# A two-layer decoder trunk on one core: HGRN operands formed two levels ahead, ScalarE reordered around the local softmax, the memory scaling moved to the local rope, the first two output tiles interleaved

## What is computed

```
hq,hf,hi,hg,rq,rk,rv,rg,sq,sk,sv,gates = split(rmsnorm(x) @ w_in)
A: HGRN2: f = lb+(1-lb)*sigmoid(hf); log_f = log(f); k = (1-lb)*sigmoid(-hf); q = silu(hq)
   o = gated linear recurrence (q, k, hi, cumulated log_f); rmsnorm(o) * silu(hg)
B: retention (q, k with rope, fixed decay); rmsnorm(o) * silu(rg)
C: sliding-window attention with rope, 128 wide, a sink per head
x += (g_a*A@w_a + g_b*B@w_b + g_c*C@w_c) @ w_out
x += cross_attention(rmsnorm(x), rmsnorm(mem))      # 256 memory tokens
x += peer_ffn(rmsnorm(x))                           # top-16 of product keys, 16384 experts
```

## Time and profile before

| | |
|---|---|
| runs, median (lowest to highest) | 2420.35 us (2418.95 to 2420.59) |
| the profiled execution's own time | 2419.26 us |
| its span, first to last instruction | 2417.5 us |
| TensorE busy | 2385.2 us, 99% |
| VectorE, ScalarE, GpSimd busy | 1646.6, 1318.2, 1097.3 us |
| chain that ended last | TensorE 89%, VectorE 8%, ScalarE 2% |

### The profile page before, as it was taken

How to read it: one execution, slowest core, us unless ns; L and a number is a source line. 1 busy time by engine, 2 the same in 40 slices (tenths; PEclk the granted TensorE clock), 3 DMA queues, 4 the chain that set the end, 5 groups by cost and what they waited for, 6 DMA issues and landing times.

```text
span 2417.5 us, 43862 instructions
## 1 busy us (share of the span) xinstructions
PE 2385.2 (99%) x15876; PEld 2168.0 (90%) x15876; DVE 1646.6 (68%) x3223; ACT 1318.2 (55%) x2048; POOL 1097.3 (45%) x452
## 2 busy tenths in 40 slices
PE   9999999999999999999999999999999999999999
PEld 8999888999999888888889898889999998888887
DVE  7467634879995556777664686258799946667776
ACT  5575555565555555554555655555555545555444
POOL 5776777787773000000067767767877730000000
PEclk9999999999999999999999999999999999999999
DMA  7544555456767667777654445544567776667775
GB/s 240 169 140 140 172 170 164 158 182 216 241 241 253 208 207 225 245 244 245 206 190 155 148 140 173 176 157 157 182 218 242 255 231 205 213 225 238 245 246 169
DMA packets 186554, 485.37 MB, mean 201 GB/s; under 512 B 14272, under 2 KB 81088, under 8 KB 181824
## 3 DMA queue, kind: packets, MB, share of 16 engines
q1 hardware_dynamic: 179808, 443.26, 55.4%
q10 hardware_dynamic: 6624, 40.44, 4.9%
HBM read 449.04 MB, written 34.60 MB: 200 GB/s over the span
## 4 chain that ended last, share of the span: by engine, by line
PE 89%; DVE 8%; ACT 2%; issue 1%; DMA 0%; SPq 0%; DVEq 0%
PE banks L894 29%; PE banks L493 13%; PE banks L495 13%; PE banks L494 13%; PE banks L836 5%; PE banks L522 5%; PE banks L865 3%; PE banks L837 3%; PE banks L523 2%; DVE arena L1692 1%; DVE arena L1738 1%; DVE arena L1690 1%; PE banks L797 1%; PE banks L781 1%; PE banks L762 1%
## 5 line engine op out<-in xcount | busy, mean ns | idle before, releaser
L423 POOL TENSOR_TENSOR w_lo<-ring,w_hi 128x1024 fp32r<-128x1024 f32 x448 | 1097.1, 2457 | 861.9 <-ACT w_hi L925 861.1
L925 ACT ACTIVATE w_hi<-ring 128x1024 fp32r<-128x1024 f32 x776 | 818.8, 1056 | 431.5 <-PE banks L894 338.6
L493 PE MATMUL banks<-h_r,w_hi 128*128 128x256 f32 x2464 | 702.5, 285 | 6.8 <-ACT arena L1000 5.6
L495 PE MATMUL banks<-h_r,w_lo 128*128 128x256 f32 x2464 | 697.0, 283 | 0.0
L494 PE MATMUL banks<-h_r,w_hi 128*128 128x256 f32 x2464 | 696.9, 283 | 0.0
L894 PE MATMUL banks<-w_hi,o_r 128*128 128x512 f32 x2048 | 559.8, 390 | 0.0
L493 PEld LDWEIGHTS banks<-h_r,w_hi 128*128 128x128 f32 x2464 | 472.0, 192 | 10.6 <-issue 8.8
L494 PEld LDWEIGHTS banks<-h_r,w_hi 128*128 128x128 f32 x2464 | 472.2, 192 | 0.6 <-issue 0.5
L495 PEld LDWEIGHTS banks<-h_r,w_lo 128*128 128x128 f32 x2464 | 472.1, 192 | 0.0
L894 PEld LDWEIGHTS banks<-w_hi,o_r 128*128 128x128 f32 x2048 | 380.0, 188 | 79.4
L1945 DVE TENSOR_TENSOR w_lo<-ring,w_hi 128x1024 fp32r<-128x1024 f32 x320 | 390.0, 1219 | 31.4 <-ACT w_hi L925 31.4
(11 more groups left out here) (303 smaller groups left out, 3219.6 us busy)
## 6 DMA issues: line engine op xcount, KB each, us to landing
ring<-in_stream SPq DMA_DIRECT2D x776, 512.0 KB, 3.3
gates_dram<-o_f ACTq DMA_DIRECT2D x32, 1024.0 KB, 5.5
o_f<-gates_dram SPq DMA_DIRECT2D x32, 1024.0 KB, 7.2
arena<-in_mem ACTq DMA_DIRECT2D x2, 1024.0 KB, 10.3
arena<-in_keys ACTq DMA_DIRECT2D x2, 1024.0 KB, 7.0
arena<-in_c_decay ACTq DMA_DIRECT2D x2, 768.0 KB, 5.0
x<-in_x SPq DMA_DIRECT2D x4, 256.0 KB, 5.8
out_dram<-arena SPq DMA_DIRECT2D x4, 256.0 KB, 2.1
```

The source lines that it names most:

```text
L423: pool.tensor_tensor(w_lo[:, s, :], ring[:, s, :], w_hi[:, s, :], ALU.subtract).then_inc(sem(f"low{s}"), 1)
L493: pe.matmul(out, lhs[0], rhs[0], start=first, stop=False)
L495: return pe.matmul(out, lhs[1], rhs[0], start=False, stop=last)
L925: act.activation(w_hi[:, s, :], ring[:, s, :], ACT.Copy).then_inc(sem(f"high{s}"), 1)
```

## The change

It has four parts. The core of the diff:

```diff
-        left = part(0, 4 * T)
-        right = part(1024, 4 * T)
-        operands = ((left, right), (part(7680, 4 * T), part(8704, 4 * T)))
+        operands = ((part(11776, 4 * T), part(6656, 4 * T)), (part(7680, 4 * T), part(8704, 4 * T)))
 # TensorE
+                def wide_two(g, n, src, pairs):
+                    for s, chunks in ((0, (0, 1, 2, 3, 4, 5)), (1, (0, 1, 2, 3)), (0, (6, 7)), (1, (4, 5, 6, 7))):
+                        if chunks[0] == 0:
+                            wait_tile(g, s)
+                            bank_free(n + s)
+                        for k in chunks:
+                            if k % 2 == 0:
+                                ev(pairs, k // 2 + 1, KC // 2)
...
                 group(G_RG, T_RG, feature_tile, hr)
+                if l == 0:
+                    pe.wait_ge(sem("angles"), 4)
+                    rms_sums(square, KC, sem("mem_squared"), 1, bank[:, 6, 0:T]).then_inc(sem("mem_summed"), 1)
...
                 token_group(G_HI, T_HI, hr)
                 ev("ret_out")
-                if l == 0:
-                    rms_sums(square, KC, sem("mem_squared"), 1, bank[:, 6, 0:T]).then_inc(sem("mem_summed"), 1)
...
-                with pe.Fori(0, 2) as i:
-                    for s in range(SLOTS):
-                        wide_tile(G_OUT + i, s, T_OUT + i * SLOTS + s, h_r, pairs=None if s else "mixed_low")
+                wide_two(G_OUT, T_OUT, h_r, "mixed_low")
+                for s in (2, 3):
+                    wide_tile(G_OUT, s, T_OUT + s, h_r)
+                group(G_OUT + 1, T_OUT + SLOTS, wide_tile, h_r)
 # ScalarE (the square and the root of the memory move to the retention gate, RG)
                 split_next(G_HI, 0)
                 window_exp(0)
-                split_next(G_HI, 1)
                 token_half(0, G_HI, P_HI, lambda t: hi[:, t, :])
-                split_next(G_HI, 2)
-                token_half(1, G_HI, P_HI, lambda t: hi[:, t, :])
+                token_half(1, G_HI, P_HI, lambda t: hi[:, t, :], split=False)
+                for s in range(1, SLOTS):
+                    split_next(G_HI, s)
                 copied(T_HI)
-                for n, (dst, src, scale) in enumerate(((cum, hf, 1.0), (kin, hf, -1.0), (qin, hq, 1.0))):
...
+                evac(G_HG, 0, hg[:, 0:1, :])
+                gate_sigmoid(cum, hf, 1.0)
+                gate_sigmoid(kin, hf, -1.0)
+                evac(G_HG, 1, hg[:, 1:2, :])
+                gate_sigmoid(qin, hq, 1.0)
                 window_turned(0)
-                evac_group(G_HG, by_feature(hg))
+                evac(G_HG, 2, hg[:, 2:3, :])
+                evac(G_HG, 3, hg[:, 3:4, :])
                 window_out(0)
...
+                gate_out(0)
+                ev("forget")
+                act.activation(cum, cum, ACT.Ln).then_inc(sem("log_forget"), 1)
+                gate_out(1)
+                window_exp(1, (0, 1))
+                gate_out(2)
+                window_exp(1, (2, 3))
+                gate_out(3)
+                level_exp(1)
+                gate_out(4)
+                gate_out(5)
+                window_turned(1)
+                gate_out(6)
+                level_exp(2)
+                gate_out(7)
+                window_out(1)
+                ahead_of = {0: 3, 3: 4, 5: 5, 7: 6, 9: 7, 10: 8}
                 for q in range(12):
-                    if q % 3 != 2:
-                        level_exp(q // 3 * 2 + 1 + q % 3)
+                    if q in ahead_of:
+                        level_exp(ahead_of[q])
                     gate_out(8 + q)
 # VectorE
                 dve.tensor_tensor(st, bank[:, 0:4, 0:3 * P], decay, ALU.mult).then_inc(sem("ret_decayed"), 1)
+                if l == 0:
+                    dve.wait_ge(sem("mem_rooted"), 1)
+                    link(dve.reciprocal(minv[:, :], minv[:, :]))
...
+                scaled_mem(range(KC // 2))
                 out_of_banks(T_HF)
...
                 rope(wqk, ...).then_inc(sem("win_roped"), 1)
+                scaled_mem(range(KC // 2, KC))
...
                 window_softmax(1, first_span)
+                level_operands(1)
+                level_operands(2)
                 window_low(1)
                 link(take_level(0))
+                for i in range(3, 9):
+                    link(take_level(i - 2))
+                    level_operands(i)
+                link(take_level(7))
```

More of the change, by code:

```diff
@@ L524, in wide_tile @@
                     m.then_inc(sem(f"slot{s}_used"), 1)
+                def wide_two(g, n, src, pairs):
[6 more added lines that the diff above has]
+                                ev(pairs, k // 2 + 1, KC // 2)
+                            hi, lo = weights(s, k)
+                            pe.matmul(wide_out(s), hi, src[:, :, k, :], start=(k == 0), stop=False)
+                            m = pe.matmul(tile_out(s), lo, src[:, 0, k, :], start=False, stop=(k == KC - 1))
+                        if chunks[-1] == KC - 1:
+                            m.then_inc(sem(f"slot{s}_used"), 1)
                 def token_group(g, n, src):
@@ L703, in level_across @@
                     ev("level_ready", 9, 9)
+                    lt, rt = operands[0]
                     for hd in range(HEADS):
-                        m = pe.matmul(bank[:, 2, hd * P:(hd + 1) * P], left[:, hd * T:hd * T + P],
-                                      right[:, hd * T + P:(hd + 1) * T], start=True, stop=True)
+                        m = pe.matmul(bank[:, 2, hd * P:(hd + 1) * P], lt[:, hd * T:hd * T + P],
+                                      rt[:, hd * T + P:(hd + 1) * T], start=True, stop=True)
                     m.then_inc(sem("level_scored"), 1)
@@ L1024, in by_feature, with token_half @@
                     return lambda n: dst[:, bass.ds(n, 1), :]
-                def token_half(t, g, n, dst):
+                def token_half(t, g, n, dst, split=True):
                     if t == 0:
@@ L1032, in token_half @@
                     act.activation(dst(t), bank[:, 4 + t, :], ACT.Copy).then_inc(sem("bank_free"), 1)
-                    if t:
+                    if t and split:
                         high_part(l * GROUPS + g + 1, SLOTS - 1)
@@ L1049, in _ @@
                 act.activation(cosb[:, 1, :], cosb[:, 1, :], ACT.Sin).then_inc(sem("trig"), 1)
+                if l == 0:
+                    act.wait_ge(sem("mem_summed"), 1)
+                    act.activation(minv[:, :], bank[:, 6, 0:T], ACT.Sqrt, bias=eps[:, :], scale=1.0 / D
+                                   ).then_inc(sem("mem_rooted"), 1)
                 copied(T_SQ)
@@ L1675, in first_span, with level_operands @@
                     span_of(1)
[L1677 to L1687 removed]
+                def level_operands(i):
+                    m = LEVELS[i]
                     ev("level_exp", 2 * i, 16)
@@ L1735, in _ @@
                 link(dve.tensor_tensor(summed, summed, hgs, ALU.mult))
-                ev("mem_loaded", 16, 16)
-                for k in range(KC):
-                    dve.scalar_tensor_tensor(mem[:, k, :], mem[:, k, :], gain["xkv"][:, k:k + 1], minv[:, :],
-                                             ALU.mult, ALU.mult).then_inc(sem("mn_made"), 1)
                 ev("hgrn_rooted")
```

47 lines of the change are left out of this document (14 added, 33 removed).

## The result

The changed kernel takes 2443.9 us (median, 2443.06 to 2445.03), the kernel before 2420.2 beside it: a ratio of 1.0099, 95% interval 1.0082 to 1.0117. It is slower by 23.7 us, where 9.7 were predicted, and lies above the predicted range. The profiled execution took 2445.03 us, its span is 2443.2.

The account below looks back on a forecast made before the run. TensorE, 99% busy, bounds the kernel, so only its waits move the time. +3.3 (moved matmuls) + 1.55 - 0.7 (HI to level 0) + 6.0 (loop) - 0.9 (BR1) = +9.25, plus 0.5 for clock: 2430 us, range 2408 to 2439.

Parts of the forecast that it names:

- two kinds: TensorE's waits: tiles waiting for ScalarE's copy out of a bank (5.6 us), levels waiting for VectorE's second operand (3.5 us).
- Part 1, the forget chain: Around the softmax: chain ends 37.5 us behind HI's start; HI to level 0 takes 59.6 us in each layer.
- The first wait: TensorE at gate tile 3 waits 3.1 us for its bank, freed behind the logarithm and `gate_out(1)`.
- the second: TensorE at gate tile 4 waits 3.15 us more, its bank freed behind half of the exponentials and `gate_out(2)`.
- Part 2, the memory: Moved sums of squares cost +3.3 us behind RG; BR1's third tile waits 0.45 us less, 0.9 in both layers.
- Part 3, the loop: Level loop with operands formed ahead: between -3.3 and +5.4 us, taken as +3.0 in each layer.
- ties: Level loop: +5.4 us if all go to GpSimd; half could go the other way, at 2.3 us each.
- The clock: TensorE's lower clock behind long waits: 0.5 us added in all.
- Part 4, the output tiles: Interleaved output tiles: the mixture's third low part is asked for at the same chunk, so 0 us, at most 0.1.
- My own rule from part 1: VectorE and GpSimd's port pair is locked for a whole instruction; a VectorE instruction with two SBUF inputs waits.
- (c): Rival: full collisions and the lower clock, both waits in one layer behind each other: +16.9 us, 2437; chance 0.13.
- (a): Rival: VectorE gets between GpSimd's instructions, neither gate tile waits, HI to level 0 takes 53.2 us, 2405; chance 0.2.

Follow-up runs that it names:

- g: Changed kernel with both interleaved output tiles' sums taken before VectorE's low parts of memory chunks 2 and 3: 2443.9 us, ratio 1.0100 to the kernel before.
- e: Changed kernel with half of each of GpSimd's low parts left out (512 of 1024 columns formed): 2401.2 us, ratio 0.9921 to the kernel before.
- h1: Changed kernel with each of GpSimd's low parts formed by two instructions of 512 columns, nothing left out: 2425.0 us, ratio 1.0023 to the kernel before.
- b: Kernel before with only the first two output tiles interleaved as in the change: 2429.5 us, ratio 1.0041.
- v2: Kernel before with output tiles interleaved in turns of four chunks, sums first, one memory low part behind each sum: 2418.9 us, ratio 0.9994.
- h2: Kernel before with each of GpSimd's low parts formed by two instructions of 512 columns: 2418.9 us, ratio 0.9997.
- v4: Kernel before with gate tile copies ahead, output tiles interleaved in turns of four chunks, and GpSimd's low parts halved everywhere: 2413.9 us, ratio 0.9974.
- d: Kernel before with only the memory's squares, sums, root and scaling moved to where the change has them: 2423.9 us, ratio 1.0015.
- a: Changed kernel without the interleaving, all output tiles one after the other: 2434.3 us, ratio 1.0060 to the kernel before.

## Why the prediction was wrong, point by point

- *TensorE's waits alone move the time, and they are of two kinds.* Right, with a third kind added by the change: a wait for VectorE's sum of an output tile.
- *Part 1, the forget chain.* Right. The forget gate was forecast 37.5 us behind HI's start; ScalarE's logarithm starts at 1367.23 in layer 1, and HI at 1330.01: 37.2. At the head of the chain there are three instructions of 2.3 to 2.5 us, and one of 3.30 later:

```profile
1351.74 0.80 DVE L1664 TENSOR_SCALAR arena<-arena,oml,low 128x256 f32<-128x256 f32 x1 [8.90 <-ACT arena L1123]
1352.46 2.48 DVE L1666 TENSOR_SCALAR arena<-arena,oml 128x256 f32<-128x256 f32 x1
1354.98 2.33 DVE L1664 TENSOR_SCALAR arena<-arena,oml,low 128x256 f32<-128x256 f32 x1
1357.23 2.48 DVE L1666 TENSOR_SCALAR arena<-arena,oml 128x256 f32<-128x256 f32 x1
...
1361.90 3.30 DVE L1669 SCALAR_TENSOR_TENSOR arena<-arena 128x1024 f32<-128x1024 f32 x1
```

  The stretch was forecast at 59.6 in each layer and took 59.28 and 59.21. The first wait was 2.9 (3.1 forecast), the second 1.55 (3.15): the tiles between them ran partly at the lower clock, which took up the difference. That the stretch came out right is so in part luck: the second wait was twice too long, and the clock of this place was put at nothing.
- *Part 2, the memory.* Right: 3.4 us for the moved matmuls (3.3), 0.40 and 0.39 at branch 1 (0.45 each). The other 1.2 us of the front lie in its first 64 us, where runs of one and the same code differ by as much.
- *Part 3, the loop.* The sequence was right at its head: span 2 was to be ready 2 us behind level 0's start (2.1 by the timeline) and span 3 at +8.5 (8.1), and tile 10 was to wait 2 us (1.8). Followed row by row it gave +5.4 in each layer. The step that failed is the choice behind it: I discounted that to +3.0, because half of the ties could go the other way. They didn't: nine of VectorE's instructions took over 2 us where four did. Measured +5.97 and +6.03, and +5.22 in the one loop without a stretch at half clock (g, layer 1).
- *The clock*, "0.5 in all". Failed, by its size. It is within the stretches above: about 0.8 us in each loop and about 1.2 at each output, 4 us in these four places by an estimate from g's layers.
- *Part 4, the output tiles*, "0 us; at most 0.1 either way". This failed outright, and with 9.3 to 9.6 us it is the largest error. I looked at what tile 0 waits for and not at what two tiles that end together release: two splits, two of GpSimd's low parts in one piece, and under them the only instructions of VectorE there with two inputs in SBUF. My own rule from part 1 was at hand.
- *The rivals.* (c) came nearest, 2437 by full collisions and the clock; with part 4's 9.6 it would have been 2446. (a) did not happen: its 53.2 us for both stretches appear only in e, where GpSimd has half of the work (53.14 and 53.16, and 2401). Its 2405 also lay below the range of 2408 to 2439 that was to take in most of it.

The Trainium skill, "SBUF — State Buffer", section "Who interferes with whom", on which the prediction drew, calls the port pair an exclusive lock in which one engine blocks the other for a whole instruction rather than sharing. The halves (h1: more work for GpSimd, 19 us less time) agree with it. Its rule that the order of issue decides who blocks is not tested here by itself: b and v2 have the same instructions in another order and lie 5.8 us apart in one stretch, but v2's order also spreads VectorE's low parts over GpSimd's pauses.

What stays open: why halves shorten the long remainders by 0.7 to 1.8 us each (h1, h2 and v4 alike; not looked into), what the operands two levels ahead cost without ScalarE's new order in the loop, and whether the operands two levels ahead would pay with halves and an order of ScalarE made for them (h1's layer 1 loop took 47.30, under the 47.87 of before, its layer 0 loop 48.79).

## What to carry to other kernels

Where an engine can be held for a whole instruction of another, count collisions, not busy time: VectorE pays about once for each of GpSimd's instructions that it is running under, so an edit that moves VectorE's work to where GpSimd runs without a pause, or that makes two of GpSimd's instructions come in one piece, costs microseconds at places that the edit doesn't name. Ask of any reordering of matmul tiles what their ends release, and in what order the engines behind take it. And when a row-by-row sequence of the trace gives a number, don't halve it because some ties might fall better. A wait of about 3 us on TensorE mostly brings a stretch at half clock; price it at its place, since it cost 1.2 us where TensorE set the pace and 0.8 us at most where VectorE did.

## What the runs showed of the hardware

- GpSimd's 128x1024 subtraction takes 2.46 us on average, the 128x512 one 1.32: two halves cost 0.19 us more, and less time overall where VectorE meets every one of them.
- A 0.69 us instruction of VectorE that waits for one of these takes up to 2.90 us, and two of 0.4 us took 4.61 under two of them: in a run of GpSimd's instructions without a pause, VectorE got one of its own done for each of them.
- In the changed kernel every late start of TensorE of 2.8 us or more (six) was followed by 3.41 us at a granted clock of 0.50. It isn't so each time: over the traces of all kernels here it was 25 of 28. The three others are one of 3.1 us in d (at 159.96) and two in g of 3.3 and 2.9 us (at 299.00 and 1428.26). Of six late starts of 1.8 us four were followed by one (the changed kernel, a and g).
- With GpSimd's instructions half as long and no wait in the loops (e) the mean clock was 1.000 over the span, in the changed kernel 0.995.
- Sixteen matmuls, 3.3 us of TensorE, were free where they stood and cost 3.4 us elsewhere, although the kernel before shows no wait of that size there: the wait they covered appears only in the other layer, and in d.
